# Other PSUM banks for a feed-forward half's first result, added terms ahead of value products, and decay rows in two fp32r parts

## The chip, the cores and the metric

The kernel runs on one core of a Trainium2 chip. The metric is device microseconds of one execution, the median of several. The kernel is one program of some 40,000 instructions on five engines: TensorE (PE, its weight loads PEld), VectorE (DVE), ScalarE (ACT), GpSimd (POOL) and the queue that issues the weight transfers (SP).

## What is computed

Two transformer blocks of two layers each, on 256 tokens of width 1024, all in fp32:

```python
# first block, layer l
y_sb = stick_breaking_attention(q_sb, k_sb, v_sb)              # 8 heads of 64
log_f = log_sigmoid(f_pre + b_f)                               # one row of 256 per head
cum_f = cumsum(log_f)
logits = where(k_pos <= q_pos, q.k/8 + cum_f[t] - cum_f[s], -inf)   # decay attention, 8 heads
x = x + (g_sb*y_sb@w_o_sb + g_fx*y_fx@w_o_fox) @ w_out
h = rmsnorm(x)
x = x + (silu(h@w_g) * (h@w_u)) @ w_dn          # layer 0, dense, width 2816; layer 1: top-2 of 8 experts

# second block, layer l (256 tokens and 256 context tokens; the last layer drops the context outputs)
# mLSTM branch, grouped-query attention branch, neighbourhood attention branch:
s_win = q.k/8 + position_bias                   # window of 8 x 16, plus the context keys
x = x + ga1 * rms_norm(merge(...))
u = conv3(h @ w_up); x = x + ga2 * rms_norm((a * silu(g)) @ w_down)   # width 2816
```

In the decay attention the term `cum_f[t]` is the same for a whole row of logits and drops out of the softmax; what is added is `-cum_f[s]` for each key, and the causal mask.

## The kernel before

**Products.** Nearly every matrix product is made of three fp32r products: operands are split into an upper and a lower part (`w_hi`, `w_lo`, `h_hi`, `h_lo`, `act_hi`, `act_lo`), and hi·hi, hi·lo and lo·hi are added up in PSUM. A weight unit is up to 128 x 1024 elements: SyncE loads it into `raw` (4 places), ScalarE rounds it into `w_hi` (L1097), VectorE subtracts to get `w_lo` (L1626; 3 places each), TensorE uses both. Units are split two ahead of the one in use. Some small products take plain fp32 operands; the trace shows each non-transposing fp32 product as two records.

**Feed-forward stages.** There are three with the mode `ffn`: the dense one of the first block (`evac="swiglu"`, 256 columns, two tiles of tokens) and one in each layer of the second block (`evac="conv"`; layer 0 with 512 columns and four tiles, layer 1 with 256 and two). Each goes through two halves of the width (`it` = 0, 1). A half has 13 results q: 0 to 10 are up results (`FB` = 11), each of two units, gate and value, in the PSUM banks b and b + 1, made in L2488; 11 and 12 are down results (L2501), one tile of tokens a bank from b on, of six units each. b is `4 * (q % 2)` everywhere: in the use by TensorE (`use`), and in the saving by ScalarE and VectorE (`save`). Before a result opens, TensorE waits on `results_saved`: for results with q > 0, until all but the last one are saved (`alternates`); for q = 0 of the second half, with 13 results an odd number, until all of them are saved, q = 12 too. q = 12 is saved by VectorE (L1672 into `o` or L1675 into `x_tm`). Between the up units of the dense stage and of layer 0, units of the modulation weights are used (`use_mod`, L2442), whose results stand in bank 2.

**Attention stages.** The steps of an attention ride along with the weight units of other products: `attend` is called with k = 0 to n + 2 on TensorE, ScalarE and VectorE, and a step lies between the tiles of a unit. Items go in pairs (the two heads of a 128-wide chunk). For the softmax modes, TensorE's step k turns the probabilities of item k − 2 (`turn`, L2869, bank 6); if k is even, it makes the value products of the pair k − 4 (`pair_gather`, L2889, bank 7, each head into 64 of the 128 output rows), and then the scores of the pair k (`pair_scores`, banks 4 and 5): first the added terms (L2855), then q·k (L2858, 64 rows of contraction). The scores wait on `exp_done`, that the exponentials of the pair before are done. VectorE takes the maximum (L2200), ScalarE the exponentials (L1445), VectorE normalizes (L2215, L2216), ScalarE copies the turned probabilities out (L1465), and splits off the upper part of the output (L1477), VectorE the lower (L2249).

Added terms stand in two attentions. The decay attention of the first block (16 items in each of two layers; pairs with 128 and with 256 keys in turn) adds `row_of` times the decay rows, an fp32 product, and the identity times the causal mask, an fp32r product. `row_of_b` has ones in row h and in row 32 + h for head h; `row_of` is the same memory read as fp32. The neighbourhood attention of the second block adds the identity times the position bias (fp32, 256 columns) for the items of the 256 main tokens: in layer 0 for 16 of 32 items, none of them in the first two pairs, in layer 1 for all 16. The stick-breaking and the grouped-query attention have none.

**Decay rows.** They come from `head_norm` on VectorE: step 0 clears `rows[:, 3]`, 128 x 256; step 8 makes log sigmoid (L2041), its cumulative sum (L2042) and the negation (L2043), on 8 partitions, and counts up `heads_ready`. TensorE's `turn_heads` (L2674), which turns q and k of the decay attention, waits for that.

```python
            def pair_scores(i):                                      # cut
                if st.mode == "stick" and i:
                    pe.wait_ge(bounded, st.at["bounded"] + i)
                else:
                    pe.wait_ge(exp_done, k0 + i)
                for j in range(adds):
                    for e, z in pair:
                        mm(z[:, 0:n_add], lhs, rhs, start=j == 0, stop=False)
```

Of the kernel before, what the change touches and what calls it, by code (L numbers as in the profile page):

```python
# [5 lines left out]
F32 = mybir.dt.float32  # L6
# [3 lines left out]
ALU = mybir.AluOpType  # L10
# [3 lines left out]
P = 128  # L14
# [101 lines left out]
class Segment:  # L116
# [74 lines left out]

    def result(self, it, q):
        return it * self.results + (self.result0 + q)
# [32 lines left out]
def build(nc, a, out):  # L226
    ctx = ExitStack()
    with ctx:
# [79 lines left out]
        row_of_r = rounded("row_of_r", Y_AT + 4 * T, ML_H, P)  # L308
        ring = [view(at, UNIT) for at in [6400 + i * UNIT for i in range(6)] + [14848 + i * UNIT for i in range(2)]]
# [328 lines left out]
        def first_layer(l, before, ctx_turned):  # L638
# [43 lines left out]
            for dt in range(2):  # L682
# [7 lines left out]
                                       add=[(row_of[:, 2 * pr + hh, :], rows[:, 3, 0:(t + 1) * P], None),  # L690
# [373 lines left out]
        def _(act):  # L1064
# [34 lines left out]
            def save(seg, it, j):  # L1099
# [10 lines left out]
                b = 4 * (q % 2)  # L1110
# [492 lines left out]
        def _(dve):  # L1603
# [31 lines left out]
            def save(seg, it, j):  # L1635
# [5 lines left out]
                b = 4 * (q % 2)  # L1641
# [320 lines left out]
            def head_norm(st, j):  # L1962
# [13 lines left out]
                if j == 0:  # L1976

                    dve.wait_ge(half_saved[0], st.at["half0"])
                    dve.wait_ge(half_saved[1], st.at["half1"])
                    if st.rope:  # L1980
                        dve.wait_ge(pv_done, st.at["item"])
                    if st.rows is not None:
                        settled(nc.vector.memset(st.rows[:, 3, :], 0.0))
# [53 lines left out]
                if j == 8 and st.rows is not None:  # L2037

                    u, lf, l, neg = (st.rows[0:NH, i, 0:T] for i in range(4))
                    dve.wait_ge(stage_act, st.at["a"] + 1)  # L2040
                    settled(nc.vector.scalar_tensor_tensor(lf, u, 0.0, l, ALU.min, ALU.subtract))  # L2041
                    settled(nc.vector.tensor_tensor_scan(l, ones[0:NH, 0:1].to_broadcast([NH, T]), lf, 0.0, ALU.mult, ALU.add))  # L2042
                    nc.vector.tensor_scalar(neg, l, -1.0, None, ALU.mult).then_inc(heads_ready, 1)  # L2043
# [382 lines left out]
        def _(pe):  # L2426
# [4 lines left out]
            def use_mod(seg, it, j):  # L2431
                q, k, m, opens, closes, width, source = seg.units[j]
                i, r = seg.mod_unit(it, j), -1 - q
                if r == 0 and opens:
                    pe.wait_ge(cond_ready, 1)
                    pe.wait_ge(mod_saved, seg.at["mod"] + it)
                pe.wait_ge(mods_loaded[i % MOD_PLACES], 16 * (i // MOD_PLACES))
# [8 lines left out]
            def use(seg, it, j, first):  # L2446
                q, k, m, opens, closes, width, source = seg.units[j]
                b = 4 * (q % 2)
# [3 lines left out]
                if opens:  # L2452
                    if q == seg.down + 1 and seg.mod_rows is not None:
                        pe.wait_ge(mod_saved, seg.at["mod"] + it + 1)

                    if q == seg.down + 1 and seg.tail is not None and seg.tail.rows is not None and it == seg.iters - 1:
                        pe.wait_ge(mods_done, seg.tail.at["mods"] + 1)
                    alternates = q > 0 or seg.results % 2 == 0 and not first
                    pe.wait_ge(seg.sig.results_saved, seg.result(it, q) - (1 if alternates else 0))
# [362 lines left out]
            def attend(st, k):  # L2822
# [17 lines left out]
                def pair_scores(i):  # L2840
# [4 lines left out]
                    n_add = T if adds and nk > T else nk  # L2845
                    if st.mode == "stick" and i:
# [3 lines left out]
                    for j in range(adds):  # L2850
                        for e, z in pair:
# [3 lines left out]
                            mm(z[:, 0:n_add], lhs, rhs, start=j == 0, stop=False)  # L2855
                    for lo, hi in ([(0, nk)] if n_add == nk else [(0, n_add), (n_add, nk)]):
# [45 lines left out]
                if st.mode == "soft":  # L2902
                    if 2 <= k <= n + 1:
                        turn(k - 2)
                    if k % 2 == 0 and k >= 4:
                        pair_gather(k - 4)
                    if k % 2 == 0 and k < n:
                        pair_scores(k)
                    return
                if k % 2 == 0 and k < n:  # L2910
                    pair_scores(k)
# [105 lines left out]
```

## Time and profile before

| | us |
|---|---|
| median of 3 runs | 2747.91 (2747.39 to 2748.07) |
| the profiled execution | 2751.55 |
| its span, first to last instruction | 2749.8 |
| TensorE busy | 2630.7 (96%), 14708 products |
| VectorE, ScalarE busy | 1667.3 (61%), 1383.0 (50%) |
| mean granted TensorE clock | 0.985 of full speed |

In the rows of the trace a line such as `134.52 1.03 PE L2855 MATMUL ps<-arena,row_of_b 128*128 128x256 f32 x4` reads: start, duration, engine, line, operation, output and inputs, the part of the array that is used (rows of contraction by output rows), output shape, and how many records are merged. In square brackets at the end stands the engine's idle time ahead of it and who ended that. The ends of products are modelled: one product's duration holds the way through the array, so successive products overlap in the rows.

### The profile page before, as it was taken

To read this page: it belongs to the slowest core of one execution; us is meant where nothing else is said; L and a number is where in the kernel's file an instruction comes from. 1 tells how busy PE (TensorE), PEld (TensorE's weight loads), DVE (VectorE), ACT (ScalarE), POOL (GpSimd) and SP (SyncE) were. 2 spreads that over 40 slices of the span, in tenths; PEclk is the share of its full clock that TensorE was granted. 3 is DMA by queue.
4 is the path that set the end of the run, shared out by engine and by line. 5 is a ranking of instruction groups with operands and counts; after the bars stand their busy time and mean duration, and the time that the engine had idled before them with its cause. 6 is when DMAs were issued, how large, how long until landed. Compare 5 with 4: busy or idle time off the path is not lost.

```text
span 2749.8 us, 40432 instructions
## 1 busy us (share of the span) xinstructions
PE 2630.7 (96%) x14708; PEld 2136.2 (78%) x14708; DVE 1667.3 (61%) x2516; ACT 1383.0 (50%) x2241; POOL 103.9 (4%) x112
## 2 busy tenths in 40 slices
PE   8999999998999999999999999999999899999998
PEld 7778888676888888778876777778777678667997
DVE  5755445656998999445555544653454457456776
ACT  5645335654777777434435453532333534545655
POOL 2000001000000000000000100100000110010000
PEclk9999999999999999999999999999999899999999
DMA  7439895435899998332331223463553244334464
GB/s 227 133 114 274 253 310 157 131 123 177 302 322 333 323 318 311 94 77 62 85 88 54 74 63 129 123 181 120 153 167 101 77 108 132 98 100 138 142 188 154
DMA packets 353482, 448.05 MB, mean 163 GB/s; under 512 B 19872, under 2 KB 198176, under 8 KB 353312
## 3 DMA queue, kind: packets, MB, share of 16 engines
q1 hardware_dynamic: 349792, 435.44, 50.6%
q0 software_dynamic: 3232, 9.97, 1.3%
q8 instruction: 108, 1.77, 0.3%
q14 instruction: 62, 0.51, 0.1%
q10 hardware_dynamic: 288, 0.36, 0.0%
HBM read 444.63 MB, written 1.08 MB: 162 GB/s over the span
## 4 chain that ended last, share of the span: by engine, by line
PE 85%; DVE 7%; ACT 4%; issue 3%; POOL 0%; DVEq 0%; POOLq 0%; ACTq 0%
PE ps L2501 21%; PE ps L2488 18%; PE ps L2549 17%; PE ps L2562 8%; PE ps L2553 4%; PE ps L2858 2%; PE ps L2869 2%; PE ps L2570 2%; PE ps L2889 2%; PE ps L2757 2%; PE ps L2442 2%; DVE w_lo L1626 1%; PE ps L2855 1%; PE ps L2588 1%; ACT w_hi L1097 1%
## 5 line engine op out<-in xcount | busy, mean ns | idle before, releaser
L1626 DVE TENSOR_TENSOR w_lo<-raw,w_hi 128x1024 fp32r<-128x1024 f32 (+1 forms) x578 | 686.1, 1198 | 540.5 <-ACT w_hi L1097 455.5
L1097 ACT ACTIVATE w_hi<-raw 128x1024 fp32r<-128x1024 f32 (+1 forms) x578 | 589.7, 1030 | 325.0 <-PE ps L2501 128.2
L2549 PE MATMUL ps<-w_hi,h_hi 128*128 128x512 f32 (+1 forms) x992 | 403.6, 409 | 12.8 <-DVE h_lo L2114 6.5
L2549 PE MATMUL ps<-w_hi,h_lo 128*128 128x512 f32 (+1 forms) x992 | 380.0, 385 | 0.0
L2488 PE MATMUL ps<-h_hi,w_hi 128*128 128x256 f32 (+1 forms) x1008 | 301.6, 324 | 5.0 <-DVE arena L1672 3.7
L2562 PE MATMUL ps<-w_lo,h_hi 128*128 128x512 f32 (+1 forms) x992 | 298.4, 385 | 0.0
L2488 PE MATMUL ps<-h_lo,w_hi 128*128 128x256 f32 (+1 forms) x1008 | 297.0, 320 | 0.0
L2549 PEld LDWEIGHTS ps<-w_hi,h_hi 128*128 128x128 f32 x992 | 187.4, 189 | 71.2 <-issue 31.8
L2488 PEld LDWEIGHTS ps<-h_hi,w_hi 128*128 128x128 f32 x1008 | 192.2, 191 | 36.7 <-issue 16.1
L2562 PEld LDWEIGHTS ps<-w_lo,h_hi 128*128 128x128 f32 x992 | 183.6, 189 | 39.5
L2549 PEld LDWEIGHTS ps<-w_hi,h_lo 128*128 128x128 f32 x992 | 187.5, 189 | 29.5 <-issue 1.0
L1626 DVE TENSOR_TENSOR w_lo<-arena,w_hi 128x1024 fp32r<-128x1024 f32 (+1 forms) x192 | 201.6, 1085 | 7.6 <-ACT w_hi L1097 7.1
L2501 PE MATMUL ps<-w_hi,act_hi 128*128 128x512 f32 x520 | 204.9, 394 | 0.0
L2501 PE MATMUL ps<-w_hi,act_lo 128*128 128x512 f32 x520 | 202.6, 390 | 0.0
L2488 PEld LDWEIGHTS ps<-h_lo,w_hi 128*128 128x128 f32 x1008 | 192.4, 191 | 13.1
L1097 ACT ACTIVATE w_hi<-arena 128x1024 fp32r<-128x1024 f32 (+1 forms) x192 | 175.3, 947 | 23.5 <-PE ps L2501 22.9
L2488 PE MATMUL ps<-h_hi,w_lo 128*128 128x256 f32 (+1 forms) x1008 | 177.2, 318 | 0.0
L2488 PEld LDWEIGHTS ps<-h_hi,w_lo 128*128 128x128 f32 x1008 | 149.8, 191 | 13.1
L2501 PE MATMUL ps<-w_hi,h_hi 128*128 128x512 f32 (+1 forms) x384 | 145.7, 379 | 2.7 <-issue 2.3
L2501 PE MATMUL ps<-w_lo,act_hi 128*128 128x512 f32 x520 | 147.3, 394 | 0.6
L1445 ACT ACTIVATE arena<-ps,att 128x512 f32<-128x512 f32 (+2 forms) x128 | 72.6, 568 | 144.7 <-DVE att L2200 144.7
L2501 PE MATMUL ps<-w_hi,h_lo 128*128 128x512 f32 (+1 forms) x384 | 142.8, 372 | 0.0
(316 smaller groups left out, 4185.9 us busy)
## 6 DMA issues: line engine op xcount, KB each, us to landing
raw<-in_w_in SPq DMA_DIRECT2D x196, 512.0 KB, 3.7
arena<-in_w_mod SPq DMA_DIRECT2D x96, 512.0 KB, 5.4
raw<-in_w_up SPq DMA_DIRECT2D x88, 512.0 KB, 4.7
raw<-in_w_gu_exp SPq DMA_DIRECT2D x64, 512.0 KB, 5.7
arena<-in_w_gu_exp SPq DMA_DIRECT2D x64, 512.0 KB, 5.0
arena<-in_w_gu_exp SPq DMA_DIRECT2D x64, 384.0 KB, 4.0
arena<-in_w_dn_exp SPq DMA_DIRECT2D x48, 512.0 KB, 6.3
raw<-in_w_gu_dense SPq DMA_DIRECT2D x44, 512.0 KB, 7.6
```

Of the source, the lines that this page charges most:

```text
L1097: nc.scalar.activation(w_hi[:, half, 0:n], place[:, 0:n], ACT.Copy).then_inc(seg.sig.hi_ready, 1)
L1445: nc.scalar.activation(prob[:, i0 % 2, 0:nk], z, ACT.Exp, bias=att[:, i0 % 2:i0 % 2 + 1], accum_out=att[:, 2 + i0 % 2:3 + i0 % 2]).then_in ...
L1626: nc.vector.tensor_tensor(w_lo[:, half, 0:n], place[:, 0:n], w_hi[:, half, 0:n].bitcast(F32), ALU.subtract).then_inc(seg.sig.lo_ready, 1)
L2442: ins = mm(ps[at:at + 32, 2, 0:2 * P], cond[:, k + c, COND - 2 * r:COND - 2 * r + 32], w[:, c * width + h * 2 * P:c * width + (h + 1) * 2 ...
L2488: ins = mm(dst, w[:, f0:f0 + wide], x[:, k + c, 0:seg.N], start=upper and k + c == 0 and x is ah, stop=not upper and k + c == DC - 1)
L2501: ins = mm(dst, x, w[:, c * width:(c + 1) * width], start=upper and opens and c == 0 and x is xh, stop=not upper and closes and c == m - 1)
L2549: ins = mm(ps[:, 2 * h + p % 2, 0:width], x[:, k + c, p * P:(p + 1) * P], wh[:, c * width:(c + 1) * width], start=opens and c == 0 and x i ...
L2553: ins = mm(ps[0:wide, 2 * h + p % 2, 0:seg.N], wh[:, f0:f0 + wide], x[:, k + c, 0:seg.N], start=opens and c == 0 and x is ah, stop=False)
L2562: ins = mm(ps[:, 2 * h + p % 2, 0:width], ah[:, k + c, p * P:(p + 1) * P], wl[:, c * width:(c + 1) * width], start=False, stop=last and no ...
L2570: ins = mm(ps[0:wide, 2 * h + p % 2, 0:seg.N], wl[:, f0:f0 + wide], ah[:, k + c, 0:seg.N], start=False, stop=last)
L2757: ins = mm(ps[0:wide, bank, cols_], w[:, f0:f0 + wide], x[:, k + c, cols_], start=begins and kind == 0, stop=ends and kind == 2)
L2858: ins = mm(z[:, lo:hi], e["q"], e["k"][:, lo:hi], start=lo == 0 and not adds, stop=hi == nk)
```

## The change

Three edits.

1. `Segment.base(it, q)` gives the first PSUM bank of a result and is 6 for q = 0 of the second half of a feed-forward stage, `4 * (q % 2)` otherwise. With that, q = 0 counts as alternating in the second half too, so it waits for all results but the last. The first modulation unit of the second half waits until q = 12 of the half before is saved.
2. `pair_scores` is cut in two: `pair_adds` with the waits and the added terms, and the rest. In the softmax modes a pair that has added terms has them ahead of the value products; the other pairs keep their order.
3. The decay rows are kept as fp32r: the upper part in rows 0 to 7 and the lower in rows 32 to 39 of `decay_parts`, which lies where the fourth of the old rows was. One fp32r product with `row_of_b` adds both.

```diff
+    def base(self, it, q):
+        return 6 if self.mode == "ffn" and it and q == 0 else 4 * (q % 2)
...
+        DECAY_LO = 32
+        decay_parts = rounded("decay_parts", 18432 + 3 * T, T)
...
-                                       add=[(row_of[:, 2 * pr + hh, :], rows[:, 3, 0:(t + 1) * P], None),
+                                       add=[(row_of_b[:, 2 * pr + hh, :], decay_parts[:, 0:(t + 1) * P], None),
...
@@ save (ScalarE), save (VectorE), use (TensorE)
-                b = 4 * (q % 2)
+                b = seg.base(it, q)
...
@@ head_norm (VectorE)
-                        settled(nc.vector.memset(st.rows[:, 3, :], 0.0))
+                        settled(nc.vector.memset(decay_parts.bitcast(F32), 0.0))
...
-                    u, lf, l, neg = (st.rows[0:NH, i, 0:T] for i in range(4))
+                    u, lf, l = (st.rows[0:NH, i, 0:T] for i in range(3))
...
-                    nc.vector.tensor_scalar(neg, l, -1.0, None, ALU.mult).then_inc(heads_ready, 1)
+                    hi = decay_parts[0:NH, :]
+                    settled(nc.vector.tensor_scalar(hi, l, -1.0, None, ALU.mult))
+                    nc.vector.scalar_tensor_tensor(decay_parts[DECAY_LO:BIAS_K, :], l, -1.0, hi.bitcast(F32), ALU.mult, ALU.subtract)\
+                        .then_inc(heads_ready, 1)
...
@@ use_mod (TensorE)
                     pe.wait_ge(mod_saved, seg.at["mod"] + it)
+                    if it:
+                        pe.wait_ge(seg.sig.results_saved, seg.result(it, 0))
...
@@ use (TensorE)
-                    alternates = q > 0 or seg.results % 2 == 0 and not first
+                    alternates = q > 0 or not first and (seg.results % 2 == 0 or seg.mode == "ffn")
...
@@ attend (TensorE)
-                def pair_scores(i):
+                def pair_of(i):
 
                     pair = [(st.items[i + hh], ps[:, 4 + (k0 + i + hh) % 2, :]) for hh in range(2)]
                     nk = pair[0][0]["nk"]
                     adds = len(pair[0][0]["add"])
                     n_add = T if adds and nk > T else nk
+                    return pair, nk, adds, n_add
+
+                def pair_adds(i):
+
+                    pair, nk, adds, n_add = pair_of(i)
                     if st.mode == "stick" and i:
                         pe.wait_ge(bounded, st.at["bounded"] + i)
                     else:
...
                             mm(z[:, 0:n_add], lhs, rhs, start=j == 0, stop=False)
+
+                def pair_scores(i):
+
+                    pair, nk, adds, n_add = pair_of(i)
                     for lo, hi in ([(0, nk)] if n_add == nk else [(0, n_add), (n_add, nk)]):
...
                 if st.mode == "soft":
                     if 2 <= k <= n + 1:
                         turn(k - 2)
+                    if k % 2 == 0 and k < n and st.items[k]["add"]:
+                        pair_adds(k)
                     if k % 2 == 0 and k >= 4:
                         pair_gather(k - 4)
                     if k % 2 == 0 and k < n:
+                        if not st.items[k]["add"]:
+                            pair_adds(k)
                         pair_scores(k)
                     return
                 if k % 2 == 0 and k < n:
+                    pair_adds(k)
                     pair_scores(k)
```

## Rows read from the trace of the kernel before

**Rows 1.** The page, part 4: shares of the chain that ended last.
```profile
PE 85%; DVE 7%; ACT 4%; issue 3%; POOL 0%; DVEq 0%; POOLq 0%; ACTq 0%
```

**Rows 2.** Waits of TensorE: who waited for whom, total us, times, longest.
```profile
PE ps L2869 <- DVE arena L2216: 15.6, 15, 3.1
...
PE ps L2674 <- DVE arena L2043: 3.2, 2, 1.6
```

**Rows 3.** Timeline, TensorE at the half of layer 0's feed-forward stage.
```profile
1928.72 1.07 PE L2501 MATMUL ps<-w_lo,act_hi 128*128 128x512 f32 x4
1932.17 0.50 PE L2488 MATMUL ps<-h_hi,w_hi 128*128 128x512 f32 x1 [2.38 <-DVE arena L1672]
1932.51 0.40 PE L2488 MATMUL ps<-h_lo,w_hi 128*128 128x512 f32 x1
...
1936.39 0.39 PE L2488 MATMUL ps<-h_lo,w_hi 128*128 128x512 f32 x1
```

**Rows 4.** Windows: busy (x count) of PE, PEld, DVE, ACT, POOL; granted clock; DMA.
```profile
1933.00:1936.00 3.00, 3.00 (x8) 2.30 (x7) 0.25 (x1) 0.00 (x0) 0.00 (x0) 0.50 0.00 0
```

**Rows 5.** Timeline, TensorE behind the dense stage's and the last layer's boundary.
```profile
337.39 0.39 PE L2488 MATMUL ps<-h_hi,w_hi 128*128 128x256 f32 x1 [1.33 <-DVE x_tm L1675]
...
2647.56 0.39 PE L2488 MATMUL ps<-h_hi,w_hi 128*128 128x256 f32 x1 [1.33 <-DVE arena L1672]
```

**Rows 6.** Timeline, ScalarE's and VectorE's splits ahead of layer 0's boundary.
```profile
1928.97 1.06 ACT L1097 ACTIVATE w_hi<-raw 128x1024 fp32r<-128x1024 f32 x1 [2.57 <-PE ps L2501]
...
1927.18 1.22 DVE L1626 TENSOR_TENSOR w_lo<-raw,w_hi 128x1024 fp32r<-128x1024 f32 x1 [4.21 <-PE ps L2501]
```

**Rows 7.** Timeline, TensorE, decay attention, a step without value products.
```profile
134.41 0.27 PE L2869 MATMUL ps<-ident,arena 128*128 128x128 f32 x1
134.52 1.03 PE L2855 MATMUL ps<-arena,row_of_b 128*128 128x256 f32 x4
135.20 0.58 PE L2855 MATMUL ps<-causal,ident_r 128*128 128x256 f32 x2
```

**Rows 8.** Timeline, TensorE, two steps with value products, 128 and 256 keys.
```profile
140.72 0.38 PE L2869 MATMUL ps<-ident,arena 128*128 128x128 f32 x2
141.03 0.44 PE L2889 MATMUL ps<-arena 128*64 128x128 f32 x4
141.40 0.71 PE L2855 MATMUL ps<-arena,row_of_b 128*128 128x128 f32 x4
...
146.82 0.66 PE L2889 MATMUL ps<-arena 128*64 128x128 f32 x8
147.41 1.13 PE L2855 MATMUL ps<-arena,row_of_b 128*128 128x256 f32 x4
```

**Rows 9.** Groups by form: line, names, shape, count | busy us, mean ns | idle.
```profile
L2855 PE MATMUL ps<-arena,ident 128*128 128x256 f32 x64 | 18.8, 419 | 0.0
...
L2855 PE MATMUL ps<-arena,row_of_b 128*128 128x256 f32 x32 | 8.8, 399 | 0.0
...
L2855 PE MATMUL ps<-arena,row_of_b 128*128 128x128 f32 x32 | 5.6, 299 | 0.9 <-ACT arena L1392 0.9
```

**Rows 10.** Timeline, ScalarE and TensorE around one even step of the decay attention.
```profile
172.01 0.19 ACT L1445 ACTIVATION_READ_ACCUMULATOR arena<-ps,att 128x1 f32 x1
172.16 0.33 PE L2869 MATMUL ps<-ident,arena 128*128 128x128 f32 x1 [0.66 <-DVE arena L2216]
...
173.18 0.28 ACT L1465 ACTIVATE arena<-ps 128x128 f32<-128x128 f32 x1 [0.98 <-PE ps L2889]
175.51 0.47 ACT L1445 ACTIVATE arena<-ps,att 128x256 f32<-128x256 f32 x1 [2.05 <-DVE att L2200]
```

**Rows 11.** Timeline, VectorE: the decay rows are made.
```profile
120.34 0.41 DVE L2041 SCALAR_TENSOR_TENSOR arena<-arena 8x256 f32<-8x256 f32 x1
120.78 0.68 DVE L2042 TENSOR_TENSOR_SCAN arena<-ones,arena 8x256 f32<-8x256 f32 x1
121.50 0.28 DVE L2043 TENSOR_SCALAR arena<-arena 8x256 f32<-8x256 f32 x1
```

More of the change, by code:

```diff
@@ L1640, in save @@
                 r = seg.result(it, q)
-                b = 4 * (q % 2)
+                b = seg.base(it, q)
                 if seg.evac == "experts":
@@ L2447, in use @@
                 q, k, m, opens, closes, width, source = seg.units[j]
-                b = 4 * (q % 2)
+                b = seg.base(it, q)
                 if q < 0:
```

## Prediction

> **What bounds the kernel now.** I read the page first: 85% of the chain that ended last is TensorE [rows 1]. So a microsecond taken off TensorE's own instructions, or off a place where it stands idle, is a microsecond of the span, unless the next wait on that engine takes it back. Next the waits with TensorE as the waiting engine: the change touches three of them, the wait for the softmax of an attention item (15.6 us in 15 places), the wait for the decay rows (3.2 us in 2), and the wait at the half of the feed-forward stages [rows 2, 3]. Last the timeline around each edited place, to count what one step of it costs. I use two measures there. For products merged into one row, (duration − duration of one) / (count − 1) is the spacing: (1.07 − 0.39) / 3 = 0.227 us for 512 columns [rows 3]. And start + duration is the end of a run; the difference of two ends is what the later run costs.
>
> **Part 1, the other PSUM banks for the first up result of the second half.** There are three feed-forward stages (dense, second block's layer 0 and layer 1), each with one boundary between its two halves. There the last down result (q = 12) and the next up result (q = 0) share banks 0 and up, so TensorE waits until VectorE has taken the former out. Layer 0: the last four products start at 1928.72, so the last of them at 1928.72 + 3 × 0.227 = 1929.40, and the next could start at 1929.63; it starts at 1932.17, behind L1672 [rows 3]. That is 2.54 us. The second product follows 0.34 us later where 0.227 is usual, so restarting costs another 0.11: together 2.65 us. (The trace's own "2.38 idle" counts from the modelled end of the last product.) Behind it the granted clock is 0.50, that is 1.2 instead of 2.4 GHz [rows 4]: from 1932.51 to 1936.39 ten products start in 3.88 us, at full clock 10 × 0.227 = 2.27, so 1.61 us more. Nothing near it gives TensorE another reason to stand still, so I take this stretch as part of the stall and gone with it; not counting it is the lower end. In the dense stage and in the last layer two tiles are taken out instead of four and the idle time is 1.33 us each [rows 5]; with the 0.27 by which 2.65 exceeds 2.38, 1.60 us each. The next products there have the usual duration, so no low clock follows.
> What is late next, once the wait is gone: the weight halves of the first two units. ScalarE's split that starts at 1928.97 was released by the unit TensorE has in hand, and that is the one three units on; VectorE's lower half at 1927.18 is that of the second unit on [rows 6]. Both are ready before the boundary, and these two units are 2 × 24 products, 10.9 us of work at 0.227, while the copy of q = 12 (2.3 us) and the next split (1.2 us) run. q = 1 lies in bank 4, whose user was saved long before; the new wait ahead of the modulation products asks for the same copy, 11 us after it was due. So nothing takes it back. Part 1: 2.65 + 1.61 + 1.60 + 1.60 = 7.5 us; lower end 5.9.
>
> **Part 2, the added terms ahead of the value products.** Three kinds of products with different shapes follow each other in an even step: probabilities turned (L2869, 128 rows by 128 columns of the array), value products of the pair before last (L2889, 128*64), added terms (L2855, 128*128), scores (L2858, 64*128). With no value products between, the turn ends at 134.41 + 0.27 = 134.68 and the four passes of the terms at 135.55: 0.87 us [rows 7]. With value products between, these end at 147.48 and the same four passes at 148.54: 1.06 us [rows 8]. The change of shape costs 0.19 us. The neighbourhood attention's terms are four passes of the same shape and width a pair [rows 9]. New order: turn and terms have one shape and stand together, then value products, then scores, so one change of shape in three is gone. The step from terms to value products isn't in the trace; its nearest row is that from turn to value products, of the same two shapes, 141.47 − 141.10 = 0.37 us for four products, and I take it as equal to what it replaces. Bounds: if it cost one change more, the gain would be 0; if the order spared a second one, 0.38 a pair.
> The Trainium skill, "TensorEngine Tiling (Array Packing)", Key Properties, says that a change of tiling mode drains TensorE, while another tile of the same mode doesn't. By it the terms-to-values step pays like the turn-to-values step whatever the types, and the sum is the one I take; if the rule held for every change of operand type too, the gain would stay, since the number of those changes is the same in both orders.
> How often: the terms with the decay rows are 32 + 32 records, four a pair, so 16 pairs; those with the position bias 64 records, 16 pairs [rows 9]. Without value products ahead are the first two pairs of each decay attention (4) and of the last layer's neighbourhood attention (2). 32 − 6 = 26 pairs × 0.195 = 5.1 us.
> The terms' wait for the exponentials (exp_done) now stands ahead of the value products and could hold them. The latest case: exponentials end at 172.20 while the turn starts at 172.16 and ends at 172.49 [rows 10]; so no wait. What the value products now hold up is ScalarE's copy of the turned probabilities, which needs their buffer: it starts at 173.18, released by L2889, and ScalarE then stands idle for 2.05 us until 175.51 [rows 10]. It will come up to 4 × 0.217 = 0.87 us later; cover 2.05 us, so nothing. Without that cover it would be up to 0.87 a pair.
>
> **Part 3, the decay rows as fp32r parts.** An fp32 product is two records here. 256 columns: four records a pair, 0.87 us, 0.217 each [rows 7]. The nearest fp32r product is the causal one beside it, same shape and width: its two end at 135.78, 0.23 us after the terms (0.117 each). Saved 0.87 − 0.23 = 0.63 us. 128 columns: the terms end 0.64 us after the value products (142.11 − 141.47), less 0.19 for the shape 0.45, four at 0.11 [rows 8]. The fp32 turn beside it, of one record a product, has the same spacing, (0.38 − 0.27) / 1 = 0.11, so at 128 columns the spacing is that of the weight loads; two fp32r products take 0.22, saved 0.22 us. Eight pairs each in the two layers [rows 9]: 8 × 0.63 + 8 × 0.22 = 6.8 us. Bounds: 0 (an fp32r product as slow as two passes) to 8 × (0.87 − 0.2) + 8 × (0.44 − 0.11) = 8.0.
> The Trainium skill, "TensorE: Matmul & The Clock Gate", LDWEIGHTS, gives a load's time as its columns over 1.2 GHz. An estimate from it is 0.107 us for 128 columns, so the 128-column pairs would still save 0.22 and not the 0.33 that streaming alone suggests; the 0.11 of the rows agrees.
> The cost: VectorE writes the upper part (the old negation), waits for itself, then writes the lower one, 8 × 256 again; and this op releases TensorE, which already waits 1.6 us for it. New after the negation: some 0.04 us between dependent ops (120.34 + 0.41 to 120.78) and 0.41 us, the same form as L2041 [rows 11]: 0.45 us later, twice: 0.9 us lost. The clearing of rows before is of the same size as now. Net 5.9 us.
> Are the savings of parts 2 and 3 kept? The 15.6 us of waits for softmax might swallow them. But each of these waits is counted from the scores of its own pair, or from a weight unit, and all that is saved lies before the scores: they start earlier, and the softmax with them. Only the second item of the pair before has the shorter burst between its scores and its turn. So I keep all.
>
> **Sum.** 7.5 + 5.1 + 5.9 = 18.5 us. The profiled execution took 2751.55 us around a span of 2749.8, the median is 2747.91, so the page's run is 3.6 us above it; the saving is in instructions that every run has. 2747.9 − 18.5 = 2729.4 us.
>
> **Rivals.**
> A. The softmax waits take back parts 2 and 3. For it: 15 such waits. Against it: the point of release above. Only part 1 stays and the 0.9 is lost: 2747.9 − 7.5 + 0.9 = 2741.3 us.
> B. The decay product in fp32r is as slow as the fp32 one (the change doesn't do what it says): 2747.9 − 7.5 − 5.1 + 0.9 = 2736.2 us. Against it: the causal product.
> C. Stretches of low clock move. TensorE stands 0.45 us longer ahead of L2674 twice, and everything behind starts earlier; 1.6 us is what one short stretch cost [rows 3 and 4], a doubled one 3.2. Two doubled ones: 2729.4 + 6.4 = 2735.8 us; one fewer somewhere: 2726 to 2728.
> D. Slower than before: the same mechanism at large. Fewer passes and new waits let the clock fall in the attention stages. It decides once it eats 18.5 + 5.5 = 24 us, that is 15 short stretches of 1.61 us, about one in every second pair whose order is changed: 2747.9 + 5.6 = 2753.5 us or more. Against it: the boundary stall that lowered the clock was 2.5 us long, and nothing new is near that length.
>
> **How the numbers follow.** Forecast 0.74, A 0.06, B 0.05, C 0.11, D 0.02, anything else 0.02. The range goes down to the upper bound of part 2 and one low stretch fewer (2729.4 − 3 − 3.2 = 2723), and up to B and C together with half of part 2 lost, 2738. Within 0.2% (5.5 us, about what a measurement tells from no change) lies only what is worse than A: faster 0.95, same 0.03, slower 0.02.
>
> **What would show it.** Right: no TensorE idle ahead of L2488 at the three boundaries and a granted clock of 1.00 behind the second; terms right behind L2869 at 0.87 (neighbourhood) or about 0.23 us (decay) after it, and L2889 about 0.25 us behind the last term; TensorE idle ahead of L2674 of 2.0 instead of 1.6 us. Wrong: longer waits of L2869, a term product with two records, value products waiting for exponentials, or new places of granted clock 0.5.

## The result: 16.8 us less, and the profile after

| | before | after |
|---|---|---|
| median | 2747.99 us (2747.39 to 2751.22, 4 runs) | 2731.22 us (2730.54 to 2734.86, 4 runs) |
| ratio, 95% interval | | 0.9936 (0.9922 to 0.9951) |
| profiled execution, its span | 2751.55, 2749.8 | 2730.54, 2728.8 |

The changed kernel is faster by 0.64%. The forecast was 2729.4 us, 18.5 us less than before. The same kernel was timed twice more: 2728.67 us (21.1 less than the kernel before beside it) and 2731.52 (17.5 less). Over all 14 executions its median is 2731.3.

The page of after, busy times and the shares of the chain that ended last, beside [rows 1]:

```profile
PE 2613.9 (96%) x14676; PEld 2125.0 (78%) x14676; DVE 1668.7 (61%) x2518; ACT 1384.1 (51%) x2241; POOL 104.1 (4%) x112
...
PE 85%; DVE 7%; ACT 4%; issue 3%; DMA 1%; DVEq 0%; POOL 0%; SPq 0%; ACTq 0%; POOLq 0%
```

TensorE has 32 records fewer. Sixteen pairs had four decay records each and have two now. The shares of the chain are the same, but for 1% that now goes to DMA. TensorE bounds this kernel as it did the one before.

The waits of TensorE in after, beside [rows 2] (who waited for whom: total us, times, longest):

```profile
PE ps L2889 <- DVE arena L2225: 15.6, 16, 3.0
...
PE ps L2685 <- DVE decay_parts L2051: 4.1, 2, 2.0
```

L2889 is the turning of the probabilities (L2869 before). Its waits stayed at 15.6 us, though everything ahead of them became shorter. L2685 is the turning of the heads (L2674 before). It waits 2.0 us twice instead of 1.6. No wait of the up products (L2499, L2488 before) is left in the list.

The same place as [rows 3 and 4], the half of layer 0's feed-forward stage: TensorE's timeline, and one window with the granted clock behind the counts of the five engines.

```profile
1916.16 1.07 PE L2512 MATMUL ps<-w_lo,act_hi 128*128 128x512 f32 x4
1917.07 0.39 PE L2499 MATMUL ps<-h_hi,w_hi 128*128 128x512 f32 x1
1917.30 0.39 PE L2499 MATMUL ps<-h_lo,w_hi 128*128 128x512 f32 x1
...
1919.00:1922.00 3.00, 3.00 (x15) 2.49 (x14) 1.70 (x2) 1.05 (x1) 0.00 (x0) 1.00 0.00 0
```

Four down products start at 1916.16 and the first up product at 1917.07, that is 4 × 0.227 later. There is no gap, and the clock behind it is 1.00 (2.4 GHz): the window of 3 us counts 15 products where that of [rows 4] counts 8.

The decay attention of layer 0, TensorE's timeline of after: a step without value products, one with 128 keys and one with 256, beside [rows 7 and 8]. L2871 are the added terms, L2909 the value products, L2878 the scores.

```profile
134.39 0.27 PE L2889 MATMUL ps<-ident,arena 128*128 128x128 f32 x1
134.42 0.48 PE L2871 MATMUL ps<-decay_parts,row_of_b 128*128 128x256 f32 x2
...
140.07 0.38 PE L2889 MATMUL ps<-ident,arena 128*128 128x128 f32 x2
140.21 0.42 PE L2871 MATMUL ps<-decay_parts,row_of_b 128*128 128x128 f32 x2
140.46 0.39 PE L2871 MATMUL ps<-causal,ident_r 128*128 128x128 f32 x2
140.78 0.44 PE L2909 MATMUL ps<-arena 128*64 128x128 f32 x4
141.15 0.49 PE L2878 MATMUL ps<-arena 64*128 64x128 f32 x4
...
145.49 0.33 PE L2889 MATMUL ps<-ident,arena 128*128 128x128 f32 x1 [0.19 <-DVE arena L2225]
145.59 0.50 PE L2871 MATMUL ps<-decay_parts,row_of_b 128*128 128x256 f32 x2
145.93 0.40 PE L2871 MATMUL ps<-causal,ident_r 128*128 128x256 f32 x2
146.25 0.66 PE L2909 MATMUL ps<-arena 128*64 128x128 f32 x8
146.84 0.70 PE L2878 MATMUL ps<-arena 64*128 64x256 f32 x4
```

To compare kernels I use one measure from here on: from the start of the turn to the start of the scores. The scores of the kernel before in the same two steps as [rows 8], and the turn of the second:

```profile
142.22 0.49 PE L2858 MATMUL ps<-arena 64*128 64x128 f32 x4
...
146.56 0.33 PE L2869 MATMUL ps<-ident,arena 128*128 128x128 f32 x1 [0.19 <-DVE arena L2216]
...
148.71 0.70 PE L2858 MATMUL ps<-arena 64*128 64x256 f32 x4
```

With 128 keys the measure is 142.22 − 140.72 = 1.50 us before and 141.15 − 140.07 = 1.08 after. With 256 keys it is 148.71 − 146.56 = 2.15 before and 146.84 − 145.49 = 1.35 after. So a pair gains 0.42 or 0.80 us. Predicted were 0.195 + 0.22 and 0.195 + 0.63.

The turning of the heads in layer 0, TensorE's timeline and then a window with the granted clock:

```profile
120.54 0.76 PE L2685 MATMUL ps<-ident,arena 128*128 128x128 f32 x4 [2.04 <-DVE decay_parts L2051]
...
121.53 0.63 PE L2560 MATMUL ps<-w_hi,h_lo 128*128 128x512 f32 x1
...
122.38 0.63 PE L2560 MATMUL ps<-w_hi,h_lo 128*128 128x512 f32 x1
...
122.00:123.80 1.80, 1.80 (x6) 1.31 (x5) 0.00 (x0) 0.00 (x0) 0.00 (x0) 0.50 0.47 91
```

The idle time is the 2.0 us that was forecast. Behind it the clock is 0.50 (1.2 GHz), which was not: two products later is 0.85 us later, where 0.46 is usual. The kernel before has no such stretch here.

**Where the 21.0 us between the two spans went.** I compared when TensorE ends its last product of every weight unit in the two traces. The difference changes in these places:

| stage | us | forecast |
|---|---|---|
| start-up, until the first unit | −1.9 | 0 |
| turning of the heads, layer 0 | +2.1 | +0.45 |
| decay attention, layer 0 | −4.5 | −4.6 |
| turning of the heads, layer 1 | +0.5 | +0.45 |
| decay attention, layer 1 | −4.5 | −4.6 |
| three feed-forward boundaries | −1.58, −4.29, −1.58 | −1.60, −4.26, −1.60 |
| neighbourhood attention, layer 0 | −0.9 | −1.6 |
| neighbourhood attention, layer 1 | −1.0 | −1.2 |
| all other units | −3.3 | 0 |

The rows between the first and the last add up to −15.8 us, within the interval around the −16.8 of the medians. I take the first and the last as no part of the change. The start-up differs from run to run. The other units' share is −1.1, −1.6 and −1.6 us where before has a stretch at 1.2 GHz that after lacks or has shorter (near 448, 1393 and 2448 us of before), +0.4 where the same stretch begins at another product, and +0.6 where TensorE in after waits once more for VectorE (0.55 us, near 224 us). The last of the three stretches lies inside the neighbourhood attention of layer 1, so −1.0 and −1.6 are divided there by its pairs outside the stretch. Such stretches come and go from kernel to kernel without a pattern that fits an edit: the one near 1393 stands in the profiles of six of the eleven runs. The spans differ by more than the medians because the profiled run of before was 3.6 us above its median.

### The profile page after: what moved, and what is told of

Its sections match the earlier page's. It is cut to its first block, busy times and chain, and to the rows that moved or that the text cites. A ratio compares the mean times of both kernels' runs of the same rounds, so it can differ in the third digit from the quotient of the medians.

```text
span 2728.8 us, 40372 instructions
## 1 busy us (share of the span) xinstructions
PE 2613.9 (96%) x14676; PEld 2125.0 (78%) x14676; DVE 1668.7 (61%) x2518; ACT 1384.1 (51%) x2241; POOL 104.1 (4%) x112
## 3 DMA queue, kind: packets, MB, share of 16 engines
HBM read 444.63 MB, written 1.08 MB: 163 GB/s over the span
## 4 chain that ended last, share of the span: by engine, by line
PE 85%; DVE 7%; ACT 4%; issue 3%; DMA 1%; DVEq 0%; POOL 0%; SPq 0%; ACTq 0%; POOLq 0%
PE ps L2512 21%; PE ps L2499 18%; PE ps L2560 17%; PE ps L2573 8%; PE ps L2564 4%; PE ps L2878 2%; PE ps L2889 2%; PE ps L2581 2%; PE ps L2768 2%; PE ps L2909 2%; PE ps L2453 2%; DVE w_lo L1632 1%; PE ps L2599 1%; ACT w_hi L1103 1%; PE ps L2871 1%
## 5 line engine op out<-in xcount | busy, mean ns | idle before, releaser
L2499 PE MATMUL ps<-h_hi,w_hi 128*128 128x256 f32 (+1 forms) x1008 | 300.4, 323 | 0.0
L2499 PE MATMUL ps<-h_lo,w_hi 128*128 128x256 f32 (+1 forms) x1008 | 296.0, 319 | 0.0
L2499 PEld LDWEIGHTS ps<-h_hi,w_hi 128*128 128x128 f32 x1008 | 191.6, 190 | 30.3 <-issue 16.1
L2499 PEld LDWEIGHTS ps<-h_lo,w_hi 128*128 128x128 f32 x1008 | 191.9, 190 | 13.0
L2499 PE MATMUL ps<-h_hi,w_lo 128*128 128x256 f32 (+1 forms) x1008 | 177.2, 318 | 0.0
L2499 PEld LDWEIGHTS ps<-h_hi,w_lo 128*128 128x128 f32 x1008 | 149.8, 191 | 13.1
L1471 ACT ACTIVATE arena<-ps 128x512 f32<-128x512 f32 (+2 forms) x184 | 84.0, 456 | 108.7 <-PE ps L2909 59.4
```

The lines of the kernel that those rows point to most:

```text
L1471: nc.scalar.activation(prob_t[:, i0 % 2, 0:e["nk"]], ps[:, bank, 0:e["nk"]], ACT.Copy).then_inc(pt_saved, 1)
L2499: ins = mm(dst, w[:, f0:f0 + wide], x[:, k + c, 0:seg.N], start=upper and k + c == 0 and x is ah, stop=not upper and k + c == DC - 1)
```

## The experiments

### One part alone: the banks

The changed kernel with the order of the steps and the decay rows put back. What it keeps of the change (with the use of `base` and the wait ahead of the modulation products):

```diff
+        return 6 if self.mode == "ffn" and it and q == 0 else 4 * (q % 2)
-                    alternates = q > 0 or seg.results % 2 == 0 and not first
+                    alternates = q > 0 or not first and (seg.results % 2 == 0 or seg.mode == "ffn")
```

> Part 1 alone (other banks and the shorter wait at the half of the feed-forward stages; order of terms and decay rows as before). Theory of the sum: 7.5 us less than before, 2740.5 us; TensorE idle ahead of the second half gone in three places, the low granted clock behind layer 0's boundary gone. Rival, the low-clock stretch has another cause than the stall: 5.9 us less, and a stretch of granted clock 0.5 still stands near that boundary.

Measured: 2741.64 us (10 runs) beside 2748.39 (26 runs of before), ratio 0.9975 (0.9966 to 0.9985), so −6.75 us. Unit by unit the boundaries gave −1.58, −4.27 and −1.58, together −7.4; forecast 7.5. No stretch at 1.2 GHz stands near layer 0's boundary, so the rival with 5.9 us is out. The median shows 0.7 less, within its interval of ±2.6 us.

### One part alone: the order

```diff
                     if 2 <= k <= n + 1:
                         turn(k - 2)
+                    if k % 2 == 0 and k < n and st.items[k]["add"]:
+                        pair_adds(k)
                     if k % 2 == 0 and k >= 4:
                         pair_gather(k - 4)
```

> Part 2 alone (added terms ahead of the value products; fp32 decay rows, old banks). Theory of the change of shape: 0.19 us in each of 26 pairs, 5.1 us less than before; from the trace of the changed kernel some pairs of the neighbourhood attention of layer 0 give part of it back, so 4 to 5 us less, 2743 to 2744 us. Rival, softmax waits take it back: 0 to 1 us less, and more idle time ahead of the turns of the probabilities.

Measured: 2743.79 us (11 runs), ratio 0.9984 (0.9975 to 0.9993), −4.6 us. Its step with 128 keys (here L2886 turns, L2868 are the terms, L2906 the values, L2875 the scores):

```profile
140.63 0.38 PE L2886 MATMUL ps<-ident,arena 128*128 128x128 f32 x2
140.85 0.61 PE L2868 MATMUL ps<-arena,row_of_b 128*128 128x128 f32 x4
...
141.93 0.49 PE L2875 MATMUL ps<-arena 64*128 64x128 f32 x4
```

141.93 − 140.63 = 1.30 us, against 1.50 before: 0.20, with the same products in another order. In the neighbourhood attention the pairs with value products gained 0.19 to 0.20 us each, but for one in layer 0 and one in layer 1 that gained nothing. (A third, in layer 1, lies in a stretch of low clock and can't be compared.) Those two are read below. The rival is out: TensorE waits 15.7 us for the softmax here, 15.6 before.

### One part alone: the decay rows

```diff
-                                       add=[(row_of[:, 2 * pr + hh, :], rows[:, 3, 0:(t + 1) * P], None),
+                                       add=[(row_of_b[:, 2 * pr + hh, :], decay_parts[:, 0:(t + 1) * P], None),
-                    nc.vector.tensor_scalar(neg, l, -1.0, None, ALU.mult).then_inc(heads_ready, 1)
+                    settled(nc.vector.tensor_scalar(hi, l, -1.0, None, ALU.mult))
+                    nc.vector.scalar_tensor_tensor(decay_parts[DECAY_LO:BIAS_K, :], l, -1.0, hi.bitcast(F32), ALU.mult, ALU.subtract)\
+                        .then_inc(heads_ready, 1)
```

> Part 3 alone (decay rows as two fp32r parts; old order and banks). Theory: 6.8 us less for TensorE, 0.9 us more ahead of the turning of q and k, 5.9 us less than before, 2742.1 us; 4.3 us less if a low-clock stretch follows one of the two longer idle times, as in the changed kernel's layer 0. Rival, softmax waits take it back: 0.9 us more than before. A term product in one record, 0.63 us less a pair with 256 keys and 0.22 with 128.

Measured: 2743.21 us (11 runs), ratio 0.9978 (0.9969 to 0.9987), −5.2 us. Its step with 128 keys and the turning of the heads, TensorE's timeline:

```profile
140.51 0.38 PE L2889 MATMUL ps<-ident,arena 128*128 128x128 f32 x2
...
141.78 0.49 PE L2878 MATMUL ps<-arena 64*128 64x128 f32 x4
...
120.94 0.63 PE L2685 MATMUL ps<-ident,arena 128*128 128x128 f32 x4 [2.04 <-DVE decay_parts L2051]
...
122.24 0.63 PE L2560 MATMUL ps<-w_hi,h_lo 128*128 128x512 f32 x1
```

The step takes 1.27 us instead of 1.50: 0.23 saved at 128 keys. At 256 keys each pair gained 0.63. Ahead of the decay attention of layer 0 this kernel lost 2.1 us, ahead of layer 1's 0.46. The 2.04 us idle time is there, and the products at 0.63 behind it show the low clock too. The kernels with the banks alone and with the order alone have neither. So this stretch comes with the decay rows, not with the other two parts. The three parts alone add up to 6.75 + 4.6 + 5.2 = 16.5 us; the whole change gave 16.8. Each of the three has an interval of some ±2.5 us. The steps say it more sharply: at 128 keys 0.20 from the order and 0.23 from the rows stand against 0.42 in after. So parts 2 and 3 don't disturb each other there.

### The terms split: what is the 0.19 us?

The order could save for two reasons: fewer changes of the array's shape, or the terms filling a gap behind the turn. Here the decay products stand ahead of the value products, the causal ones behind them, so there are as many changes of shape as in the kernel before, though the terms' first half still stands right behind the turn.

```diff
-                    if k % 2 == 0 and k < n and st.items[k]["add"]:
-                        pair_adds(k)
+                    split_terms = k % 2 == 0 and k < n and len(st.items[k]["add"]) == 2
+                    if k % 2 == 0 and k < n and st.items[k]["add"]:
+                        pair_adds(k, 0 if split_terms else None)
...
+                        elif split_terms:
+                            pair_adds(k, 1)
```

> The changed kernel, but in the decay attention only the first of the two terms (decay rows) stands ahead of the value products; the second (causal mask) follows them, ahead of the scores. The work is the same, but the shapes change three times a pair again (terms to values, values to terms, terms to scores), as before. Theory of the change of shape: 0.19 to 0.2 us back in each of the 12 pairs of the decay attentions that have value products, 2.3 us more than the changed kernel. Rival, the terms gain by covering a wait of the value products: the first term still covers it, so no more than 0.5 us above the changed kernel.

Measured: 2732.03 us (5 runs), ratio 0.9941 (0.9928 to 0.9955), against 2728.67 of the changed kernel beside it. TensorE's timeline of the step with 128 keys:

```profile
138.15 0.38 PE L2889 MATMUL ps<-ident,arena 128*128 128x128 f32 x2
138.29 0.42 PE L2871 MATMUL ps<-decay_parts,row_of_b 128*128 128x128 f32 x2
138.64 0.44 PE L2909 MATMUL ps<-arena 128*64 128x128 f32 x4
139.01 0.44 PE L2871 MATMUL ps<-causal,ident_r 128*128 128x128 f32 x2
139.37 0.49 PE L2878 MATMUL ps<-arena 64*128 64x128 f32 x4
```

139.37 − 138.15 = 1.22 us, 0.14 more than the changed kernel. At 256 keys it was 1.54 against 1.35, 0.19 more. Unit by unit the 12 pairs gave back some 2.0 us, 0.17 each. The kernel with the decay rows alone has the same products in the old order, with the same count of shape changes. It takes 1.27 and 1.51 us in these two steps, beside 1.22 and 1.54 here. So the gain goes with the count of shape changes; having the first term right behind the turn is worth 0.05 us at most. The medians can't settle this: this kernel is 3.4 us above the changed kernel beside it, but 0.7 above the median of all its 14 executions.

### The wait kept, the banks changed

Parts 2 and 3 and the other banks stay; only the wait of the first up result is as before.

```diff
-                    alternates = q > 0 or not first and (seg.results % 2 == 0 or seg.mode == "ffn")
+                    alternates = q > 0 or seg.results % 2 == 0 and not first
```

> The changed kernel with its new banks, but with the old wait: the first up result of the second half again waits until all results are saved. If it is the wait and what follows it, not the bank, then all of part 1 is lost: the idle times of 1.33, 2.38 and 1.33 us are back, with the granted clock of 0.5 behind the one of 2.38, 5.9 to 7.5 us more than the changed kernel. Rival, the low-clock stretch in layer 0 was not the stall's: the idle time is back without it, 5.9 us more, and the products behind the boundary at full clock.

Measured: 2738.71 us (5 runs), ratio 0.9963 (0.9950 to 0.9977), 10.0 us above the changed kernel beside it. First the list of waits, then TensorE's timeline at layer 0's boundary:

```profile
PE ps L2499 <- DVE arena L1678: 3.7, 2, 2.4
...
1924.14 0.50 PE L2499 MATMUL ps<-h_hi,w_hi 128*128 128x512 f32 x1 [2.38 <-DVE arena L1678]
...
1926.01 0.63 PE L2499 MATMUL ps<-h_lo,w_hi 128*128 128x512 f32 x1
1926.44 0.63 PE L2499 MATMUL ps<-h_hi,w_hi 128*128 128x512 f32 x1
```

The idle time is again 2.38 us, and the low clock is back behind it, products 0.43 us apart. Unit by unit the boundaries cost 1.59, 4.28 and 1.59 us, 7.5 together. The rest of the 10.0 is scatter: the changed kernel beside it came out 2.6 us below its median over all runs. This is the firmest proof for one term of the sum. The low clock behind the stall, 1.6 us, came and went with the stall: all four profiles with the 2.38 us (before, the order alone, the decay rows alone and this one) have it, and none of the seven without.

### The heads released before the decay rows

The turning of the heads doesn't need the decay rows; only the added terms do. Here `heads_ready` counts up before the rows are made, and the rows get a signal of their own, on which the first added term of the decay attention waits.

```diff
-                                       add=[(row_of_b[:, 2 * pr + hh, :], decay_parts[:, 0:(t + 1) * P], None),
+                                       add=[(row_of_b[:, 2 * pr + hh, :], decay_parts[:, 0:(t + 1) * P], (decay_ready, l + 1)),
...
+                    dve.sem_inc(heads_ready, 1)
                     u, lf, l = (st.rows[0:NH, i, 0:T] for i in range(3))
...
-                        .then_inc(heads_ready, 1)
+                        .then_inc(decay_ready, 1)
```

> The changed kernel, but the turning of q and k (L2674 of before) waits only until they are normalized, no longer for the decay rows, which get a count of their own that the first added term waits for. The idle time of 2.04 us ahead of it was the wait for the decay rows alone: it goes in both layers, about 2.2 us each with the restart, and with it the low-clock stretch behind the first (1.6 us): 4.4 to 6 us less than the changed kernel, 2725 to 2727 us. Rival, another wait ends as late (normalization, or the copies out of the turned heads): at most 1 us less than the changed kernel.

Measured: 2725.54 us (5 runs), ratio 0.9917 (0.9904 to 0.9931), 22.9 us less than before. Next to the changed kernel's ratio of 0.9936 that is not yet a difference, as the intervals overlap, so both were run again beside each other.

> The changed kernel as it is, on the same chip as the version with its own signal for the decay rows, so that the two share their neighbours. Theory (the idle time ahead of the turning of the heads, 2.04 and 1.9 us, is on the path, and a low-clock stretch of 1.6 us stands behind the first in some runs): 18.5 us below before, give or take 2, so near 2730. Rival (that idle time is given back by later waits): the same time, and no distance to the next kernel.

> The version in which the turning of q and k no longer waits for the decay rows, a second time and beside the changed kernel. Theory: 4.4 us below the changed kernel (2.2 us in each of the two layers), 6.0 where the low-clock stretch stands behind the idle time in the changed kernel. Rival (later waits take the idle time back): within 1 us of it.

Measured: the changed kernel 2731.52 us (5 runs), this one 2727.30 (5 runs), 4.2 us less. The two ratios to before overlap again, 0.9935 (0.9921 to 0.9949) and 0.9919 (0.9905 to 0.9932). Over all 14 executions of the one (mean 2731.1, scatter 1.9) and 10 of the other (2726.9, 1.6) the distance is 4.2 us, with √(1.9²/14 + 1.6²/10) = 0.72 as its standard error. In the second comparison alone, each of the five executions of this version (2729.31 at most) lies below each of the changed kernel's (2730.26 at least). From the first trace of this version, TensorE at the turning of the heads, then VectorE at the decay rows, and the wait of the first added term:

```profile
119.72 0.60 PE L2687 MATMUL ps<-ident,arena 128*128 128x128 f32 x4
...
119.89 0.41 DVE L2049 SCALAR_TENSOR_TENSOR arena<-arena 8x256 f32<-8x256 f32 x1
...
128.22 0.41 PE L2873 MATMUL ps<-decay_parts,row_of_b 128*128 128x128 f32 x2 [0.57 <-ACT arena L1399]
```

There is no idle time ahead of L2687. The decay rows are begun at 119.89, and the first term that needs them stands at 128.22 and waits for ScalarE, not for them. Between the two traces of the second comparison the units gave −3.7 us in layer 0 and −2.2 in layer 1, together −5.9; a start-up 0.4 us later and low-clock stretches that lie elsewhere leave 3.3 between the spans. The rival, that later waits take the idle time back, fails in the timeline: the difference stands behind both places. This version beats both kernels.

### The changed kernel again

> The changed kernel once more, on the chip of the two runs beside it, so that their differences to it can be read: 2731 us, 0.6% less than before. A second profile of it: the low-clock stretch behind the turning of q and k of layer 0 stands there again if it belongs to the idle time of 2.04 us; if it is chance, it may be gone.

Measured: 2728.67 us (2727.75 to 2733.04, 5 runs), ratio 0.9927 (0.9914 to 0.9941). Its 5 runs spread over 5.3 us. Of the six profiles in which TensorE stands idle for 2.04 us ahead of L2685 in layer 0, four have the low clock behind it (after, the decay rows alone, and both repetitions) and two have not (the split terms, the kept wait). By this repetition the low clock is no chance of one run, but it isn't there each time either.

## Why the prediction was right, and where it was off

**What bounds the kernel.** Right. All three parts are savings on TensorE or at its idle places, and each reached the span. Two of the prediction's own signs of being wrong did appear, and both are read below: a new place of granted clock 0.5, and pairs held up by the exponentials.

**Part 1, 7.5 us.** Right in every term: 7.45 in after, 7.4 alone, 7.5 when the wait came back. It was right to count the 0.27 us of spacing and restart beyond the 1.33 and 2.38 that the trace calls idle: three times that is 0.8 us. It was right to count the low-clock stretch behind the layer 0 boundary as part of the stall. Nothing was late next: the first products followed at 0.227 (1917.07, 1917.30), and the list of waits has none of the up products.

**Part 2, 5.1 us; measured alone 4.6.** The price of a shape change was right (0.20, and 0.14 to 0.19 when given back), and so was the choice for the unseen step: from the terms to four value products it is 141.22 − 140.85 = 0.37 us, which is what [rows 8] show from the turn to the values. The failed step is "The latest case: exponentials end at 172.20 while the turn starts at 172.16", and the "no wait" behind it. I had looked for the latest case in the decay attention only. In the neighbourhood attention two pairs are later, one in each layer. First TensorE, then ScalarE, in after, for the one in layer 0 and then for the one in layer 1:

```profile
1589.39 0.41 PE L2889 MATMUL ps<-ident,arena 128*128 128x128 f32 x2
1589.75 1.13 PE L2871 MATMUL ps<-arena,ident 128*128 128x256 f32 x4
...
1589.49 0.21 ACT L1451 ACTIVATION_READ_ACCUMULATOR arena<-ps,att 128x1 f32 x1
...
2461.06 0.66 PE L2889 MATMUL ps<-ident,arena 128*128 128x128 f32 x4
...
2461.37 0.21 ACT L1451 ACTIVATION_READ_ACCUMULATOR arena<-ps,att 128x1 f32 x1
2461.64 0.70 PE L2871 MATMUL ps<-arena,ident 128*128 128x256 f32 x2
```

In layer 0 the exponentials end at 1589.49 + 0.21 = 1589.70. The turn's two products start at 1589.39 and 1589.53, so the terms could have started near 1589.64. They start at 1589.75, and their end at 1590.88 is 1.08 us behind the turn's where 0.87 was counted. The 0.21 us of wait and restart take back the whole gain of this pair. Before, value products stood there and covered it. In layer 1 the exponentials end at 2461.37 + 0.21 = 2461.58 and the terms start at 2461.64, 0.58 us behind the start of the turn where 0.49 us is usual in this layer; from the turn to the scores that pair takes 2.66 us, as it did before (2.67), where its neighbours went from 2.67 to 2.48. The kernel with the order alone shows the same in both layers. Two of 26 pairs without their 0.195 make 24 × 0.195 = 4.7 us, near the 4.6 of the median. In after layer 0 lost another 0.25 us, for a reason that has its place in the last section.

**Part 3, 6.8 us less 0.9.** The prices were right: 0.63 and 0.22 forecast, 0.63 and 0.23 measured. The cost of VectorE's second op was right too, as its timeline in after shows:

```profile
119.67 0.28 DVE L2050 TENSOR_SCALAR decay_parts<-arena 8x256 fp32r<-8x256 f32 x1
119.98 0.41 DVE L2051 SCALAR_TENSOR_TENSOR decay_parts<-arena,decay_parts 8x256 fp32r<-8x256 f32 x1
```

From the end of the first, 119.95, to that of the second, 120.39, are 0.44 us. The idle time grew from 1.6 to 2.04. What was missing is the 1.6 us of low clock behind it in layer 0. From the first turning of the heads to the third, after takes 126.03 − 120.54 = 5.49 us; the kernel with the split terms, which has the same idle time and no low clock, takes 124.11 − 120.19 = 3.92. Rival C had this mechanism and named this wait, with a chance of 0.11. Against rival D I had written that "nothing new is near" the 2.5 us of the boundary stall; 2.04 was near enough in four profiles of six. The term should have been 0.9 plus about two thirds of 1.6. That would account for some 1.1 of the 1.7 us between 18.5 and 16.8, and the two late pairs for 0.4. But the interval of the 16.8 is ±4 us, so no distance of 1.7 is shown by the medians.

**Are the savings kept?** Yes. L2889 waited 15.6 us where L2869 had waited 15.6, and every decay pair with value products gained 0.40 to 0.42 us at 128 keys and 0.78 to 0.82 at 256. Rival A (2741.3 us) is out by this. Rival B (2736.2) is out by the 0.23 and 0.63 us of the kernel with the decay rows alone, rival D (2753.5 or more) by every run.

**The sum.** Working it from the trace gives 15.8 us for the change in this one execution. The three single parts give 16.5, the three timings of the whole change 16.8, 21.1 and 17.5. The forecast of 18.5 lies within the interval of each of the three timings (13.5 to 21.4, 16.2 to 23.6 and 14.0 to 21.7 us, by their ratios), and their mean is 18.5. That the mean meets it is luck in part: in the profiled execution the edits themselves gave 2.7 us less than forecast, and the start-up and stretches far from them gave the rest of the difference.

**What stays open.** Why the same 2.04 us of idle time is followed by 1.2 GHz in four profiles of six, and never in layer 1, no run here tells. The two without it are those in which TensorE restarts earliest in layer 0 (120.19 and 120.43 us, the other four at 120.54 or later), but the kernel before restarts at 121.93, after 1.59 us of idle time, without it. The place where the low clock begins differs: right behind the restart in after, about a microsecond behind it in the kernel with the decay rows alone.

## What to carry to other kernels

Price a stall by the starts of products on either side, with the slower product behind the restart and any stretch of low clock that follows: here 1.33 us of "idle" cost 1.60, and 2.38 cost 4.26. Put products that use the array in the same shape next to each other, as each change of shape cost 0.2 us here; and when a wait moves ahead of other work with them, look up the latest release in every stage that runs this code, not in one. Let a signal say only what its waiter needs: taking the decay rows out of the signal that releases the heads brought 4.2 us, four fifths of what the whole edit of the decay rows had brought alone (5.2).

## What the runs showed of the hardware

**An idle time of 2.04 us can be enough for 1.2 GHz, and isn't always.** Rows and count stand above. Where it comes, it costs 1.6 us more.

**A VectorE op can take four times as long beside one of GpSimd, if both start at once.** In after's neighbourhood attention, first VectorE, then GpSimd, then TensorE:

```profile
1582.67 1.48 DVE L2225 TENSOR_SCALAR arena<-arena,att 128x256 f32<-128x256 f32 x1
...
1582.68 1.31 POOL L1066 TENSOR_TENSOR arena<-arena,window 128x512 f32<-128x512 f32 x1 [2.29 <-DMA arena<-in_position_bias]
...
1584.20 0.44 PE L2889 MATMUL ps<-ident,arena 128*128 128x128 f32 x2
```

The same form took 354 ns on average in the kernel before; here it took 1.48 us, while GpSimd added the window to the position bias. It ended at 1584.15, and the turn of the probabilities followed at 1584.20, about 0.25 us late. The Trainium skill, "SBUF — State Buffer", Terms, says that VectorE and GpSimd arbitrate for one pair of ports, which the winner holds for its whole instruction. The trace fits that, as the VectorE op ended 0.16 us after GpSimd's. Overlap alone doesn't do it. In the repetition of the changed kernel, VectorE and then GpSimd:

```profile
1562.33 0.35 DVE L2225 TENSOR_SCALAR arena<-arena,att 128x256 f32<-128x256 f32 x1
...
1562.39 1.44 POOL L1066 TENSOR_TENSOR arena<-arena,window 128x512 f32<-128x512 f32 x1 [2.34 <-DMA arena<-in_position_bias]
```

VectorE started 0.06 us earlier and kept its 0.35 us; GpSimd's op took 1.44 us. In the eleven profiles this form of VectorE overlaps GpSimd's addition 22 times. In 20 of them VectorE started 0.06 us or more ahead and took 0.36 us at most; the two slow ones (1.48 here, 1.43 in the first trace with the heads released) are those in which both started within 0.03 us of each other. So the op that is clearly first keeps its time. Which one was first in the two slow cases can't be read: in one VectorE's record starts 0.01 us ahead, in the other GpSimd's 0.03 ahead. A change that only shifts the work in time can bring such a pair together or part it.
